# A hybrid decoder step on one core: output and query projections by tiles, top-k by heads

## What is computed

```python
hp = hp + mixed @ w_out                            # mixed (320, 2048), w_out (2048, 2048)
x = rmsnorm(hp, norm2_g)
qq = (x @ wq).reshape(N, 8, 2, 128)                # peer_wq (2048, 2048)
s1 = einsum('nhd,hkd->nhk', qq[:, :, 0], k1)       # 8 heads, 128 keys each
s2 = einsum('nhd,hkd->nhk', qq[:, :, 1], k2)
v1, i1 = top_k(s1, 16);  v2, i2 = top_k(s2, 16)
sc, ci = top_k(all 16 x 16 sums v1 + v2, 16)       # per token and head
e = i1[ci // 16] * 128 + i2[ci % 16]               # one of 16384 experts
g = softmax(sc)
act = gelu(einsum('nd,nhjd->nhj', x, U[e]))
hp = hp + einsum('nhj,nhjd->nd', g * act, V[e])    # U, V (16384, 2048) f32
y = rmsnorm(hp, final_norm_g)
```

## Time and profile before

| | |
|---|---|
| time, median of 3 runs | 3029.74 us (3029.67 to 3032.33) |
| profiled execution: time, span | 3028.37 us, 3026.5 us |
| TensorE busy, share of the span | 2327.3 us, 77% |
| VectorE busy | 1422.8 us, 47% |
| ACT, Pool busy | 405.8 us, 466.8 us |
| gathers | 320, 671 MB |
| other DMA | 135 MB |
| mean granted TensorE clock | 0.906 of 2.4 GHz |

### The profile page before, as it was taken

The page is one execution under the profiler, slowest core; times in us unless marked ns, Lnnn a source line. Parts: engine busy times, 40 slices in busy tenths (PEclk is TensorE's granted clock), DMA queues, the critical chain, the costliest instruction groups (busy, mean ns, idle before and its releaser), DMA issues.

```text
span 3026.5 us, 22843 instructions
## 1 busy us (share of the span) xinstructions
PE 2327.3 (77%) x8537; PEld 1416.7 (47%) x8537; DVE 1422.8 (47%) x2419; ACT 405.8 (13%) x845; POOL 466.8 (15%) x329
## 2 busy tenths in 40 slices
PE   5999997864678898891777777777777777777776
PEld 4999997433367675890223223223222222232221
DVE  3333333644210001447895895555555555555554
ACT  3222223212211001330000000001000000000000
POOL 0000000000000000000323222222222222223331
PEclk8999998765566699895999999999999999999999
DMA  4443442120032234223999999999999999999996
GB/s 124 146 146 124 146 146 68 62 82 0 11 113 85 84 111 125 87 80 132 428 410 422 428 427 401 429 427 428 429 428 428 428 428 428 427 428 429 428 427 285
DMA packets 163768, 807.01 MB, mean 267 GB/s; under 512 B 12358, under 2 KB 116610, under 8 KB 121818
## 3 DMA queue, kind: packets, MB, share of 16 engines
q0 software_dynamic: 46080, 671.11, 52.2%
q1 hardware_dynamic: 117610, 134.91, 14.0%
HBM read 795.51 MB, written 10.21 MB: 266 GB/s over the span
## 4 chain that ended last, share of the span: by engine, by line
PE 44%; DMA 36%; DVE 10%; issue 7%; ACT 1%; SPq 0%; POOL 0%; DVEq 0%; ACTq 0%; POOLq 0%
DMA rows_in<-in_peer_uv,expert 35%; PE bank L227 9%; PE bank L844 6%; PE bank L846 6%; PE bank L845 6%; PE bank L842 5%; PE bank L815 2%; PE bank L1054 2%; PE bank L1055 1%; PE bank L1038 1%; PE bank L996 1%; PE bank L951 1%; PE bank L962 1%; PE bank L822 1%; DVE diag L411 1%
## 5 line engine op out<-in xcount | busy, mean ns | idle before, releaser
L227 PE MATMUL bank<-rows_in,diag 128*128 128x512 f32 (+1 forms) x2560 | 1192.4, 610 | 453.4 <-DVE diag L411 453.4
L438 DVE CUSTOM_DVE_ANT_0 rows_in<-rows_in,x2n 128x2048 f32<-128x2048 f32 x320 | 733.6, 2293 | 643.8 <-DMA rows_in<-in_peer_uv,expert 643.1
L227 PEld LDWEIGHTS bank<-rows_in,diag 128*128 128x128 f32 (+1 forms) x2560 | 440.2, 181 | 1203.5 <-DVE diag L411 707.0
L295 POOL DMA_INDIRECT rows_in<-in_peer_uv,expert x320 | 460.5, 1439 | 1712.2 <-PE bank L227 1104.9
L1247 DVE TENSOR_TENSOR wl<-wring,wh 128x2048 fp32r<-128x2048 f32 x72 | 164.8, 2292 | 332.4 <-ACT wh L1089 332.4
L844 PE MATMUL bank<-xnh,wh 128*128 128x336 f32 x896 | 285.0, 318 | 23.2 <-DVE wl L1247 23.2
L846 PE MATMUL bank<-xnh,wl 128*128 128x336 f32 x896 | 285.2, 318 | 0.0
L845 PE MATMUL bank<-xnl,wh 128*128 128x336 f32 x896 | 284.6, 318 | 0.0
L275 ACT ACTIVATE dots<-dots 128x1 f32<-128x1 f32 x320 | 64.9, 203 | 1530.1 <-DVE dots L438 1530.0
L1089 ACT CAST wh<-wring 128x2048 fp32r<-128x2048 f32 x72 | 137.1, 1907 | 379.9 <-PE bank L846 179.8
L844 PEld LDWEIGHTS bank<-xnh,wh 128*128 128x128 f32 x896 | 169.7, 189 | 24.0 <-issue 24.0
(11 more groups left out here) (283 smaller groups left out, 1732.5 us busy)
## 6 DMA issues: line engine op xcount, KB each, us to landing
wring<-in_w_in SPq DMA_DIRECT2D x28, 2048.0 KB, 8.2
wring<-in_w_out SPq DMA_DIRECT2D x8, 2048.0 KB, 8.1
wring<-in_peer_wq SPq DMA_DIRECT2D x8, 2048.0 KB, 8.2
kpage<-in_cache_k SPq DMA_DIRECT2D x16, 512.0 KB, 5.4
vpage<-in_cache_v SPq DMA_DIRECT2D x16, 512.0 KB
rows_in<-in_peer_uv,expert POOLq DMA_INDIRECT x320, 17.9
C<-in_state_C SPq DMA_DIRECT2D x4, 1024.0 KB, 5.8
out_C_sample<-C SPq DMA_DIRECT2D x4, 1024.0 KB, 4.4
```

The lines of the kernel that those rows point to most:

```text
L227: mm = pe.matmul(acc[d][0:w, :], diag[r % ND][:, 0:w], rows_in[r % NG][:, D + 512 * d:D + 512 * d + 512], start=False, stop=(j == ROUNDS[t ...
L295: nc.gpsimd.indirect_dma_start(out=rows_in[r % NG][:], out_offset=None, in_=UV_DR, in_offset=bass.IndirectOffsetOnAxis(ap=ids[:, j:j + 1], ...
L438: nc.vector.tensor_tensor_reduce(u, u, x2n[t][:], 1.0, 0.0, ALU.mult, ALU.add, dots[t % 2][:, j:j + 1]).then_inc(S["dot_done"], 1)
```

## The change

The products of w_out and peer_wq are no longer made for all 320 tokens at once. They are made by tiles, with tokens on the output's partitions: a weight row block (128 x 1024, 512 KB, six buffers `wk`) is the moving operand. `project(0)` handles tile 0 alone: w_out, norm along the free axis, transposes (`xt`), peer_wq, transposes of the queries (`qt`), scores. The top-k goes head by head in six steps (`head_step`), each on one head's data; gathers start when head 0 of tile 0 has its ids. `project(1)` handles tiles 1 and 2 together, which read each weight again, once for both; each engine's code calls `beside()` at 80 fixed points there, which does 1.25 rounds a point (TensorE two rounds behind the others), and on VectorE two head steps as long as any are left. After these points come 24 for the heads of tile 1 (1.25 rounds a point) and 24 for those of tile 2 (one round a point). The products are plain f32 (one pass of full f32 in place of three float32r passes for the queries). The keys arrive transposed from the host. NG falls from 6 to 4, ND from 8 to 4. The accumulators are always banks 4 to 7, so the first matmul of a tile waits for `y_done` of the tile before; the final norm moves to rounds 1 to 3 of the next tile. The input rows x are loaded again (`h1`), with norm2_g and final_norm_g broadcast over partitions.

```diff
-NG, ND = 6, 8
+NG, ND, NW = 4, 4, 6
+HD = 1024
+HSTEPS = 6
+POINTS_B = 2 * KC + 3 + 4 + 2 * KC + 1 + 8
+POINTS_A = POINTS_B + 3 * PH
...
+    query_jobs = lambda t: [(("qt", t, 0), 0), (("qt", t, 1), 1), (("pS", t, 0), 2), (("qt", t, 2), 3), (("pS", t, 1), 0),
+                            (("qt", t, 3), 1), (("pS", t, 2), 2), (("pS", t, 3), 3)]
+    pair_jobs = lambda key: [((key, t, 2 * f + d), 2 * (t - 1) + d) for f in range(2) for t in (1, 2) for d in range(2)]
+    jobs += [(("wo", 0, d), d) for d in range(4)] + [(("xt", 0, q), q) for q in range(4)]
+    jobs += [(("wq", 0, d), d) for d in range(4)] + query_jobs(0)
+    jobs += pair_jobs("wo") + [(("xt", t, q), q) for t in (1, 2) for q in range(4)]
+    jobs += pair_jobs("wq") + query_jobs(1) + query_jobs(2)
...
+    def rounds_by(point):
+        return min(point * 5 // 4, ROUNDS[0]) if point <= POINTS_A else ROUNDS[0] + point - POINTS_A
...
+            for row in range(2 * KC):
+                r = 2 * KC * part + row
+                k, f = (row // 2, row % 2) if part < 2 else (row % KC, row // KC)
+                if r >= NW:
+                    half_read(r - NW)
+                sp.dma_start(wk[r % NW][:], w[P * k:P * k + P, HD * f:HD * f + HD]).then_inc(wk_in[r % NW], 16)
...
+        for t in range(2):
+            sp.dma_start(h1[t][:], xp[P * t:P * t + P]).then_inc(S["xr_in"], 16)
+        for n in range(2):
+            sp.dma_start(h1[2][TS * n:TS * n + TS, :], xs).then_inc(S["xr_in"], 16)
+        broadcast(g2, a["norm2_g"][0], "g2_in")
+        sp.dma_start(kT12[:], a["keys"].rearrange("d (n k) -> d n k", n=2 * PH)).then_inc(S["keys_in"], 16)
+        weight_rows(a["w_out"][0], 0)
+        weight_rows(a["peer_wq"][0], 1)
+        broadcast(gf, a["final_norm_g"], "gf_in")
+        weight_rows(a["w_out"][0], 2)
+        weight_rows(a["peer_wq"][0], 3)
...
+        def add_rows(r):
+            t, j = tile_of(r)
+            w = COLS[t]
+            if j == 0:
+                if t:
+                    pe.wait_ge(S["y_done"], t)
+                for d in range(4):
+                    pe.matmul(acc[d][0:w, :], ident[:, 0:w], h1[t][:, 512 * d:512 * d + 512], start=True, stop=False, skip_group_check=True)
+            pe.wait_ge(S["diag_done"], r + 1)
+            pe.wait_ge(row_in[r % NG], 16 * (r // NG + 1))
+            for d in range(4):
+                mm = pe.matmul(acc[d][0:w, :], diag[r % ND][:, 0:w], rows_in[r % NG][:, D + 512 * d:D + 512 * d + 512],
+                               start=False, stop=(j == ROUNDS[t] - 1), skip_group_check=True)
+            mm.then_inc(S["acc_done"], 1)
...
+            for f in range(2):
+                outs = [[open_bank((key, t, 2 * f + d)) for d in range(2)] for t in (1, 2)]
+                for k in range(KC):
+                    r = 2 * KC * part + KC * f + k
+                    pe.wait_ge(wk_in[r % NW], 16 * (r // NW + 1))
+                    for n in range(2):
+                        for d in range(2):
+                            mm = pe.matmul(outs[n][d][:], lhs[n][:, k, :], wk[r % NW][:, 512 * d:512 * d + 512], start=(k == 0), stop=(k == KC - 1))
+                            if k == KC - 1:
+                                close(mm)
+                    if k < KC - 1:
+                        mm.then_inc(S["wk_used"], 1)
+                    beside()
...
+        project(0, lambda: None)
+        point, done = [0], [0]
+        def beside():
+            point[0] += 1
+            while done[0] < rounds_by(point[0]) - 2:
+                add_rows(done[0])
+                done[0] += 1
+        project(1, beside)
+        while done[0] < TOTAL:
+            add_rows(done[0])
+            done[0] += 1
...
+        gate_at = {3 * h + 2: (0, h + 1) for h in range(PH - 1)}
+        gate_at.update({POINTS_B + 3 * h + 2: (1, h) for h in range(PH)})
+        gate_at.update({POINTS_A + 3 * h + 2: (2, h) for h in range(PH)})
+        def beside():
+            point[0] += 1
+            while done[0] < min(rounds_by(point[0]), TOTAL):
+                one_gelu(done[0])
+                done[0] += 1
+            if point[0] in gate_at:
+                exp_gate(*gate_at[point[0]])
...
+                if t < 2 and j % PK == 0:
+                    pool.wait_ge(S["e_done"], PH * t + j // PK + 1)
                 if r >= NG:
...
+        def head_step(t, h, u):
+            if u < 2:
+                if h % 2 == 0 and u == 0:
+                    evacuated(dve, ("pS", t, h // 2))
+                top_pair(best[:, u, :], besti[:, u, :], sc[t][:, 2 * h + u, :])
+                next_pair(best[:, u, :], besti[:, u, :], sc[t][:, 2 * h + u, :])
+            elif u == 2:
+                link(nc.vector.tensor_tensor(cand[:].rearrange("p (k j) -> p k j", k=PK), rows3(best[:, 0, :]), cols3(best[:, 1, :]), ALU.add))
+                link(nc.vector.tensor_copy(bestf[:], besti[:]))
+                top_pair(sums, pair, cand[:])
+            elif u == 3:
+                next_pair(sums, pair, cand[:])
+                nc.vector.tensor_tensor(gate[t][:, h, :], sums[:], sums[:, 0:1].to_broadcast([P, PK]), ALU.subtract).then_inc(S["best_done"], 1)
+                link(nc.vector.tensor_scalar(place[:, 0, :], pair[:], 4, None, ALU.logical_shift_right))
+                link(nc.vector.tensor_scalar(place[:, 1, :], pair[:], 15, None, ALU.bitwise_and))
+                link(nc.vector.tensor_copy(placef[:], place[:]))
+            elif u == 4:
+                key_of(0)
+            else:
+                key_of(1)
+                nc.vector.scalar_tensor_tensor(expert[t][:, PK * h:PK * h + PK], slot[:, 0, :], float(NK), slot[:, 1, :], ALU.mult, ALU.add).then_inc(S["e_done"], 1)
+                dve.wait_ge(S["gate_exp"], PH * t + h + 1)
+                link(nc.vector.reciprocal(gsum[t][:, h:h + 1], gsum[t][:, h:h + 1]))
+                link(nc.vector.tensor_scalar(gate[t][:, h, :], gate[t][:, h, :], gsum[t][:, h:h + 1], None, ALU.mult))
...
+        def one_dot(r):
+            t, j = tile_of(r)
+            dve.wait_ge(row_in[r % NG], 16 * (r // NG + 1))
+            u = rows_in[r % NG][:, 0:D]
+            nc.vector.tensor_tensor_reduce(u, u, x2n[t][:], 1.0, 0.0, ALU.mult, ALU.add, dots[t % 2][:, j:j + 1]).then_inc(S["dot_done"], 1)
+            if r:
+                diagonal(r - 1)
+            if t and j == 2:
+                row_mean(t - 1)
+            if t and j == 3:
+                row_out(t - 1)
...
+        dve.wait_ge(S["x2n_done"], 4)
+        for u in range(HSTEPS):
+            head_step(0, 0, u)
+        point, done = [0], [0]
+        left = [(0, h, u) for h in range(1, PH) for u in range(HSTEPS)]
+        def beside():
+            point[0] += 1
+            while done[0] < min(rounds_by(point[0]), TOTAL):
+                one_dot(done[0])
+                done[0] += 1
+            for _ in range(2):
+                if left:
+                    head_step(*left.pop(0))
+        project(1, beside)
+        for t in (1, 2):
+            left += [(t, h, u) for h in range(PH) for u in range(HSTEPS)]
+            while left:
+                beside()
+            if t == 2:
+                halves()
+        while done[0] < TOTAL:
+            beside()
...
+        acc = bank[4:8]
```

More of the change, by code:

```diff
@@ new lines, in project, with add_input @@
+        def project(g, beside):
+            tiles = ((0,), (1, 2))[g]
+            def add_input(t, d):
+                part = slice(512 * d, 512 * d + 512)
+                b = take(dve, ("wo", t, d))
+                give(nc.vector.tensor_tensor(h1[t][:, part], h1[t][:, part], b[:], ALU.add), ("wo", t, d))
+            dve.wait_ge(S["xr_in"], 64)
+            if g == 0:
+                for d in range(4):
+                    add_input(0, d)
+            else:
+                for f in range(2):
+                    for _ in range(KC):
+                        beside()
+                    for t in tiles:
+                        for d in range(2):
+                            add_input(t, 2 * f + d)
+            beside()
+            dve.wait_ge(S["norm_sq"], g + 1)
+            for t in tiles:
+                link(nc.vector.tensor_reduce(nst[t][:, 5:6], nst[t][:, 0:4], AX_X, ALU.add))
+                ins = nc.vector.tensor_scalar(nst[t][:, 4:5], nst[t][:, 5:6], 1.0 / D, EPS, ALU.mult, ALU.add)
+            ins.then_inc(S["norm_ms"], 1)
+            beside()
+            dve.wait_ge(S["norm_rms"], g + 1)
+            dve.wait_ge(S["g2_in"], 16)
+            for t in tiles:
+                link(nc.vector.reciprocal(nst[t][:, 5:6], nst[t][:, 4:5]))
+                for q in range(4):
+                    part = slice(512 * q, 512 * q + 512)
+                    nc.vector.scalar_tensor_tensor(x2n[t][:, part], h1[t][:, part], nst[t][:, 5:6], g2[:, part], ALU.mult, ALU.mult).then_inc(S["x2n_done"], 1)
+            beside()
+            for _ in range(2 * len(tiles) + 2 * KC + 1 + 4 * len(tiles)):
+                beside()
@@ new lines, in tail_vector @@
+        for q in range(SB):
```

(24 more changed lines are left out.)

511 lines of the change are left out of this document (227 added, 284 removed).

## The result

The changed kernel takes 3201.9 us (3199.7 to 3210.6), 1.057 times the one before (95% interval 1.055 to 1.059). Forecast was 3015, range 2980 to 3062: wrong in sign and outside the range. The first dot starts 212 us earlier, as meant; the time from it to the end grows by 394.

The account below looks back on a forecast made before the run. In the gather stage DMA was taken as full at 428 GB/s, 4.90 us a gather; in the output product TensorE was busy throughout. Terms -221 + 113 + 25 + 32 + 31 + 5 = -15 on 3029.7 gave 3015 us, range 2980 to 3062.

Parts of the forecast that it names:

- Ring of four: Last 168 rounds, without products, on four row buffers: 5.0 us a round, loss 5 us (0 to 30).
- The rival at 5.1: The ring takes 5.1 us a round wherever TensorE does not bound: +17 us, 3032, no change; chance 0.15.
- Stage A: First 100 rounds, beside the products of tiles 1 and 2: TensorE bounds, 610 us against 497, loss 113.
- the rival of rows that come late: Rows come late for TensorE in Stage A: 57 us more, 3072, or half of it, 3043; chance 0.28.
- My lower bound of 590: The first 100 rounds would take 590 us where DMA alone bounds.
- my 8 for all: Handovers of banks in Stage A, where VectorE waits for the last matmul of a half: 8 us.
- My sign for the rival: If TensorE waits for diag or for wk in Stage A, the rival of rows that come late holds.
- Stage B: 28 rounds beside the top-k heads of tile 1: VectorE bounds, loss 25 us against 139 before.
- Stage C: 24 rounds beside tile 2's heads, two head steps each: VectorE bounds, 151 us against 119, loss 32.
- Boundaries: Between tiles, the next tile can't start before row_out of the last: loss 16 and 15 us, together 31.
- Start: Way to the first dot: 1199.3 us against 1420.6, gain 221, 6 either way.
- Tail: After the last dot: 21.2 us, as before.

Follow-up runs that it names:

- Experiments 1 and 2: The kernel before the change with only its row buffers cut from six to four (3327.4 us, ratio 1.098) and to five (3038.3 us, 1.003).
- 3 and 4: The changed kernel with each diagonal right after its own dot (3025.7 us), and with a ring of six buffers from round 104 (3005.5 us).
- experiment 8: The changed kernel with diagonal at once up to round 100, six buffers from round 104, two bank sets, one head step a round for tiles 1 and 2: 2944.9 us.
- experiment 5: The changed kernel with accumulators on two bank sets, so a tile's matmuls don't wait for the final norm of the tile before: 3172.0 us, ratio 1.048.

## Why the prediction was wrong

**Ring of four: the step that failed.** "I take 8.2, since the first issue of a ring is the slowest, and so 5.0": the mechanism was named rightly (three rounds have to hold 6.6 and a landing, no slack), but the term for the landing was too short, and the loss is 151 instead of 5. Between 2300 and 2700 the landing is 10.3 us on average where I took 8.2, and from the next row's dot to the issue it frees there pass 7.2 where I took 6.6: together 17.5 for three rounds. Two things were wrong. I gave every gather nearly the shortest landing of the trace. 8.1 and 8.7 were two samples of the same case, a gather into an empty queue: one was issued after Pool had waited 8.9 us for TensorE, the other was the first of all, and the median was 17.9. And I took Pool's issue as free of VectorE. By my own terms, in a ring at 5.0 a round the issue stands 6.6 after one dot, so 1.6 into the next, and is held until 3.1; the earlier trace rows shows just that, at no cost under a full queue. In a ring without slack it costs: held gathers come 1.23 late on average. Then a loop without slack catches nothing up: the row is late, TensorE pauses, in this stretch at a granted clock of 0.91 against 1.00, and the next gather is asked for later. Experiments 1 and 2 show the size without the rest of the change, 3 and 4 that either a later deadline or two more buffers remove it. The rival at 5.1 had the same fault: it gave 17 us where 151 were measured.

**Stage A** (113, measured 141; 644.8 where I had 610, and before the change 503.5 where I had 497): TensorE's bound of 6.16 a round is confirmed with the loads gone (6.13), but with them it ran at 6.35 in rounds 40 to 89. That is the rival of rows that come late, at about half its price: points of 7.9. In the first 27 rounds it is 6.84. My lower bound of 590, where DMA alone bounds, was also added up wrongly: its terms give 577. Also the handover at point 16 cost more than my 8 for all: VectorE stood in two key lists when TensorE had ended its half, TensorE waited 9.5 us and Pool 17.2. In the timeline, the addition, TensorE's next work and the next issue:

```profile
1337.07 2.48 DVE L559 TENSOR_TENSOR h<-h,bank 128x512 f32<-128x512 f32 x4
...
1339.81 5.20 PE L267 MATMUL bank<-wk,mix 128*128 128x512 f32 x8 [9.53 <-DVE h L559]
...
1348.71 0.94 POOL L449 DMA_INDIRECT rows_in<-in_peer_uv,expert  x1 [17.22 <-PE bank L241]
```

After the dot of 1345.84 the next starts at 1357.49. My sign for the rival was that TensorE waits for diag; it does, 43 us between 1208 and 1830.

**Stage B** (25, measured 36): the immediate diagonal brings it to 166.7 and the ring of six to 161.3, so 6 to 12 of it are the ring; all repairs of experiment 8 together bring it to 144.0, 7 over before, and their shares are not separated. **Stage C** (forecast 1.31 over before a round, measured 1.13): right, and bound by VectorE as said: neither the diagonal (130.2 for the 20 rounds), nor six buffers (124.5), nor the banks (125.9) help it, and with the head steps spread it takes 102.2.

**Boundaries** (31, measured 44): the mechanism was right, the wait for row_out is 35 by experiment 5. Missing were the identities at the lower clock (6.72 for 3.5), at the first boundary a fourth dot at 18.6 instead of 14.7 to 17.3, and the open ring.

**Start** (-221, measured -212): the attention ends 3.8 us later, the first weight row comes another 1.4 late, and the second product takes 57.1 us where I had 54.6 (granted clock 0.97). The first gather is used 10.1 us after its issue, beside weight loads. I had 9.7, which counts the issue's 1.0 twice: in the earlier trace rows the 8.7 already runs from the issue's start. **Tail:** right. **The page of the Trainium skill** (DMA: Bandwidth & Descriptors, Anatomy of one DMA), whose formula gave 6.8 for a gather, would have closed the ring even more easily; the shortest landing in any run is 7.8, so the trace doesn't agree.

## What to carry to other kernels

Before taking a buffer out of a ring, write down its loop: what must pass from one landing until the buffer is asked for again, divided by the rounds in between. Don't put in the shortest transfer of a deep queue. Look also where in the beat the issue will fall, and what runs on VectorE just then. A loop that closes with nothing to spare is open, here by 0.9 us a round. One run of the old kernel with fewer buffers, like experiment 1, shows the loss before the rest of a change is written. If memory forces it, shorten the loop instead: the diagonal one round earlier was worth in the plain rounds what two buffers were (4.889 and 4.851 for 5.851). A buffer that is dead later (here the weights') can join the ring in the middle.
